# One product of 72 rows for forget sums and masks, and four gate tiles moved from the prompt to the decode

## The reference

```
u = RMSNorm(x);  z = u @ W_in          # q, k, v, forget gates, branch gates, merge gates mg
A (FoX, 8 heads):  s = q.k * scale + cum[query] - cum[key];  causal;  softmax;  @ v
B (NSA, 8 heads in 2 kv groups):  compressed + selected + window branches
   selected: importance per block of 64 keys (33 blocks), the 16 best are kept per token and group;
             a key of a block that is not kept gets -1e30 before the softmax
h = x + (sigmoid(g_A) * (A @ U_A) + sigmoid(g_B) * (B @ U_B)) @ W_out     # g_A, g_B from mg
y = h + HierMoE(RMSNorm(h))
```

## Time and profile before

| | |
|---|---|
| median of 3 runs | 2335.61 us (2333.5 to 2337.6) |
| the profiled execution, its own time | 2339.91 us |
| its span | 2337.8 us |
| TensorE (PE) busy | 2035.8 us, 87% |
| weight loads (PEld) | 1242.2 us, 53% |
| VectorE (DVE), ScalarE (ACT) busy | 532.0 and 235.9 us |
| moved by DMA | 614.98 MB, mean 263 GB/s |

### The profile page before, as it was taken

The page is one execution under the profiler, slowest core; times in us unless marked ns, Lnnn a source line. Parts: engine busy times, 40 slices in busy tenths (PEclk is TensorE's granted clock), DMA queues, the critical chain, the costliest instruction groups (busy, mean ns, idle before and its releaser), DMA issues. The chain is left out here.

```text
span 2337.8 us, 33992 instructions
## 1 busy us (share of the span) xinstructions
PE 2035.8 (87%) x13747; PEld 1242.2 (53%) x13747; DVE 532.0 (23%) x1099; ACT 235.9 (10%) x621; POOL 108.0 (5%) x124
## 2 busy tenths in 40 slices
PE   7999999999999999899999889999836786868773
PEld 7887677777767774454555556753322232323321
DVE  3545112223333441111111111100041111111112
ACT  0001111111102330000000011000000000000000
POOL 0000000000000000000000000000010211212111
PEclk9999999999999999999999999999967897888877
DMA  7664734332242229999999976323179999999998
GB/s 270 185 180 137 258 139 166 140 109 88 94 155 84 84 102 385 366 405 369 385 401 386 363 292 269 140 108 117 67 323 381 393 411 406 410 413 393 407 415 326
DMA packets 167986, 614.98 MB, mean 263 GB/s; under 512 B 31781, under 2 KB 89654, under 8 KB 132470
## 3 DMA queue, kind: packets, MB, share of 16 engines
q1 hardware_dynamic: 125742, 545.19, 60.1%
q0 software_dynamic: 22800, 45.07, 5.4%
q10 hardware_dynamic: 19288, 22.55, 3.0%
HBM read 702.95 MB, written 39.60 MB: 318 GB/s over the span
## 5 line engine op out<-in xcount | busy, mean ns | idle before, releaser
L511 PE MATMUL bank<-ut,wring 128*128 128x320 f32 x1408 | 385.6, 434 | 1.1 <-PEq L208 1.1
L511 PEld LDWEIGHTS bank<-ut,wring 128*128 128x128 f32 x1408 | 267.8, 191 | 112.0 <-issue 3.4
L1215 PE MATMUL bank<-ut,zt 128*128 128x320 f32 x576 | 180.2, 452 | 20.0 <-DMA zt<-in_w_gate 12.5
L2103 PE MATMUL bank<-wdn,par 128*32 128x512 f32 x512 | 88.7, 826 | 110.2 <-issue 108.8
L1215 PEld LDWEIGHTS bank<-ut,zt 128*128 128x128 f32 x576 | 103.1, 191 | 92.5 <-issue 46.4
L824 PE MATMUL bank<-ut,wring 128*128 128x320 f32 x448 | 144.4, 447 | 0.6 <-DVE ncum L1068 0.6
L2074 PE MATMUL bank<-wgu,arena 128*32 128x512 f32 x1024 | 119.9, 609 | 0.8 <-DVE arena L2154 0.8
L1542 PE MATMUL bank<-wring,arena 128*128 128x512 f32 x256 | 112.0, 595 | 3.1 <-DVE arena L1582 1.6
L674 DVE RECIPROCAL selmask<-selmask 128x320 f32<-128x320 f32 x30 | 64.5, 2149 | 201.3 <-ACT selmask L648 201.3
L824 PEld LDWEIGHTS bank<-ut,wring 128*128 128x128 f32 x448 | 80.8, 194 | 27.8 <-issue 7.9
L2103 PEld LDWEIGHTS bank<-wdn,par 128*32 128x32 f32 x512 | 18.2, 132 | 142.9 <-issue 141.1
(11 more groups left out here) (414 smaller groups left out, 2297.2 us busy)
## 6 DMA issues: line engine op xcount, KB each, us to landing
wgu<-in_w_gu SPq DMA_DIRECT2D x128, 1024.0 KB, 13.6
wdn<-in_w_dn SPq DMA_DIRECT2D x32, 2048.0 KB
arena<-in_kv_v SPq DMA_DIRECT2D x88, 640.0 KB, 8.6
arena<-in_kv_k SPq DMA_DIRECT2D x84, 640.0 KB, 9.1
wring<-in_w_proj SPq DMA_DIRECT2D x44, 1024.0 KB, 4.9
wring<-in_w_merge SPq DMA_DIRECT2D x32, 1024.0 KB, 4.9
wring<-in_kv_k SPq DMA_DIRECT2D x44, 640.0 KB, 9.3
wring<-in_kv_v SPq DMA_DIRECT2D x40, 640.0 KB, 9.4
```

The lines of the kernel that those rows point to most:

```text
L511: last = nc.tensor.matmul(m.bank[:, 2 + s % 2, 0:T], m.wring[:, s, k * P:(k + 1) * P], m.ut[:, k, :], start=(k == 0), stop=(k == KD - 1))
L1215: last = nc.tensor.matmul(m.bank[:, 7, 0:T], m.gw[n % 2][:, k // 2, k % 2 * P:(k % 2 + 1) * P], m.ut[:, k, :], start=(k == 0), stop=(k == ...
L2103: last = nc.tensor.matmul(m.bank[j * TW:(j + 1) * TW, 6 + i % 2, :], e.hid[:, i % 2, f * TW:(f + 1) * TW], w[:, f, cols:cols + 512], start ...
```

## The change

It does three things. (1) The score step has one product of 72 rows in place of the 16 products with `ncum` and the 4 with `maskq`: 64 rows are the turned sums (sequence, head) of a page's keys, and 8 rows tell a key's block within 512 keys. The stationary side, `extra`, is built on VectorE per sequence: ones for the sequence's own heads, and the masks of the step's 8 blocks. `ncum` is held as (page, b, head) and turned by 16 transposes and 4 copies, two on VectorE and two on ScalarE, into memory that the gate copies of the prompt used, so that both engines first wait for the stores of those. (2) The masks come out of 4 matmuls and one VectorE operation in `prompt_stage`. (3) NP is 10 in place of 14: 10 gate tiles in the prompt, 22 in the decode, and 5 matmuls of them after each step of scores and 4 after each of values.

```diff
-        self.blockof = self.selmask_all[0:NSB, :]
-        self.ncum = sb("ncum", P, NB, PAGES, FH)
+        self.cum_rows, self.block_rows = self.selmask_all[0:NB * FH, :], self.selmask_all[64:72, :]
+        self.ncum = sb("ncum", P, PAGES, NB, FH)
-        self.maskq = self.wflat[0:NSB, 7168:8192].rearrange("p (b j c) -> p b j c", b=NB, j=4)
+        self.masks = self.wflat[64:72, 7168:7168 + 4 * P]
+        self.spread = self.wflat[0:FH, 7680:7680 + FH * NT]
...
-NP = 14
+NP = 10
-SHARE = {"k": 4, "soft": 7, "v": 3}
+SHARE = {"k": 5, "soft": 7, "v": 4}
... prompt_stage, TensorE
-            done(nc.tensor.transpose(m.bank[0:NSB, 2, 0:P], rank, ident))
+            for q in range(4):
+                last = nc.tensor.matmul(m.bank[64:72, 2, q * P:(q + 1) * P], rank[:, 8 * q:8 * q + 8], ident,
+                                        start=True, stop=True)
+            done(last)
... prompt_stage, VectorE
-            nc.vector.memset(m.maskq, 0.0)
-            step(nc.vector.tensor_copy(selt[0:NSB, :], m.bank[0:NSB, 2, 0:P]))
-            for e in range(2):
-                for jj in range(2):
-                    last = nc.vector.tensor_scalar(
-                        m.maskq.rearrange("p b (g j) c -> p b g j c", g=G)[:, :, :, jj, 16 + 8 * e:24 + 8 * e],
-                        selt[0:NSB, :].rearrange("p (b g t) -> p b g t", b=NB, g=G), -NEG, NEG, ALU.mult, ALU.add)
-            step(last)
+            step(nc.vector.tensor_scalar(m.masks, m.bank[64:72, 2, :], -NEG, NEG, ALU.mult, ALU.add))
... decode_stage, SP
-            sp.dma_start(m.blockof, a["consts"][0:NSB, at:at + PAGES * P]).then_inc(m.rows_in, 16)
+            sp.dma_start(m.block_rows, a["consts"][64:72, at:at + PAGES * P]).then_inc(m.rows_in, 16)
... decode_stage, TensorE
-            for b in range(NB):
-                last = nc.tensor.transpose(m.bank[:, b // 4, (b % 4) * P:(b % 4 + 1) * P],
-                                           m.ncum[:, b, :, :].rearrange("p g h -> p (g h)"), ident)
+            for g in range(PAGES):
+                last = nc.tensor.transpose(m.bank[0:NB * FH, g // 4, (g % 4) * P:(g % 4 + 1) * P],
+                                           m.ncum[:, g, :, :].rearrange("p b h -> p (b h)"), ident)
... scores(b, q)
-                for i in range(4):
-                    for j in range(4):
-                        at = ((4 * q + i) * FH + 2 * j) * NT
-                        nc.tensor.matmul(m.bank[rows(j, 16), q, i * P:(i + 1) * P], spread[:, at:at + 16],
-                                         m.ncum[:, b, :, :].rearrange("p g h -> p (g h)"), start=False, stop=False)
                 for j in range(4):
-                    last = nc.tensor.matmul(m.bank[rows(j), q, :], m.maskq[:, b, j, :], m.blockof[:, q * 512:(q + 1) * 512],
-                                            start=False, stop=True)
+                    last = nc.tensor.matmul(m.bank[rows(j), q, :], extra[:, b % 2, q, j, :],
+                                            m.selmask_all[0:72, q * 512:(q + 1) * 512], start=False, stop=True)
...
-            pe.wait_ge(cum_ready, 3)
+            pe.wait_ge(cum_ready, 5)
... decode_stage, ScalarE
+            for s in range(2):
+                act.wait_ge(m.g_out[s], 16 * (NP // 2))
+            act.wait_ge(cum_turned, 1)
+            for x in range(2, 4):
+                nc.scalar.activation(m.cum_rows[:, x * 512:(x + 1) * 512], m.bank[0:NB * FH, x, :], ACT.Copy
+                                     ).then_inc(cum_ready, 1)
... decode_stage, VectorE, queries(b)
+                for e in range(2):
+                    nc.vector.tensor_copy(extra[0:NB * FH, b % 2, :, :, 8 * e:8 * e + 8],
+                                          bc(mine[:, :, e], NT).unsqueeze(1).broadcast_to([NB * FH, 4, 4, NT]))
+                    for jj in range(2):
+                        nc.vector.tensor_copy(extra[64:72, b % 2, :, :, 16 + 8 * e:24 + 8 * e].rearrange(
+                            "p q (g j) t -> p q g j t", g=G)[:, :, :, jj, :], masks[:, :, b, :, :])
... decode_stage, VectorE, its begin
             nc.vector.memset(qp, 0.0)
-            step(nc.vector.memset(pn, 0.0))
-            nc.vector.tensor_copy(spread.rearrange("p (n t) -> p n t", t=NT), bc(ident, NT)).then_inc(cum_ready, 1)
-            for b in range(2):
-                queries(b)
+            nc.vector.memset(pn, 0.0)
+            step(nc.vector.memset(m.snew_all[0:72, 512:1536], 0.0))
+            nc.vector.tensor_copy(m.spread.rearrange("p (n t) -> p n t", t=NT), bc(ident[0:FH, 0:FH], NT)).then_inc(cum_ready, 1)
+            queries(0)
+            for s in range(2):
+                dve.wait_ge(m.g_out[s], 16 * (NP // 2))
             dve.wait_ge(cum_turned, 1)
             for x in range(2):
-                nc.vector.tensor_copy(m.ncum[:, 4 * x:4 * x + 4, :, :].rearrange("p b g h -> p (b g h)"), m.bank[:, x, :]
-                                      ).then_inc(cum_ready, 1)
+                nc.vector.tensor_copy(m.cum_rows[:, x * 512:(x + 1) * 512], m.bank[0:NB * FH, x, :]).then_inc(cum_ready, 1)
+            queries(1)
```

More of the change, by code:

```diff
@@ L182, in __init__ @@
                          (self.onsa[:, :, :].rearrange("p h t -> p (h t)"), a[:, 12800:KVS * 1024]))
-        in_ncum = Pieces(self.ncum[:, :, :, :].rearrange("p b g h -> p (b g h)"))
+        in_ncum = Pieces(self.ncum[:, :, :, :].rearrange("p g b h -> p (g b h)"))
         self.ckt, self.part, self.hidp = in_ncum(P, G * TP), in_ncum(P, 256), in_ncum(P, 2, CW)
@@ L769, in prompt_stage @@
         (V_QSAMPLE, V_LFTOK, V_MAX, V_SHIFT, V_SUM, V_RECIP, V_PROBS, V_PCT, V_SCORE, V_FORCED,
-         V_CMP, V_TIES, V_ABOVE, V_RANK, V_SEL, V_SELT, V_MASK, V_CMPO, V_PAGESUM, V_NCN) = range(1, 21)
-        V_PAST = 21
+         V_CMP, V_TIES, V_ABOVE, V_RANK, V_SEL, V_SELT, V_CMPO, V_PAGESUM, V_NCN) = range(1, 20)
+        V_PAST = 20
         units = [(kind, h) for h in range(H) for kind in ("fox", "cmp", "slc", "win")]
@@ L1067, in _ @@
                 dve.wait_ge(pe_s, E_PAST + 2 * h + 1)
-                step(nc.vector.tensor_scalar(m.ncum[:, :, :, h], m.bank[:, (5, 1)[h % 2], 0:P].rearrange(
-                    "p (b g) -> p b g", b=NB), -1.0, None, ALU.mult))
+                step(nc.vector.tensor_scalar(m.ncum[:, :, :, h].rearrange("p g b -> p b g"), m.bank[
+                    :, (5, 1)[h % 2], 0:P].rearrange("p (b g) -> p b g", b=NB), -1.0, None, ALU.mult))
             chain = Chain(dve, back_step)
@@ L1128, in decode_stage @@
         in_vt = Pieces(m.vt[:, 0:2, :, :].rearrange("p a h d -> p (a h d)"))
-        spread = m.snew_all[:, 512:1536]
+        extra = m.snew_all[0:72, 512:1536].rearrange("p (s q j c) -> p s q j c", s=2, q=4, j=4)
         pt, ptw, ptn = in_arena(P, PAGES, P), in_arena(P, 4, P), in_arena(P, 2, P)
@@ L1256, in new_scores @@
                 for j in range(4):
-                    nc.tensor.matmul(m.bank[rows(j, 16), 4, 0:NT], spread[0:FH, 16 * j:16 * j + 16],
+                    nc.tensor.matmul(m.bank[rows(j, 16), 4, 0:NT], m.spread[:, 16 * j:16 * j + 16],
                                      m.ncn[:, b * NT:(b + 1) * NT], start=False, stop=False)
@@ L1390, in queries @@
                 q = qp[:, b % 2, :].rearrange("p (j c) -> p j c", j=4)
+                mine = ident[0:NB * FH, b * FH:(b + 1) * FH].rearrange("p (j e) -> p j e", e=2)
+                masks = m.masks.rearrange("p (q b g t) -> p q b g t", q=4, b=NB, g=G)
+                for e in range(2):
[4 more added lines that the diff above has]
+                            "p q (g j) t -> p q g j t", g=G)[:, :, :, jj, :], masks[:, :, b, :, :])
                 nc.vector.tensor_scalar(q[:, :, 0:80].rearrange("p j (e c) -> p j e c", e=2)[:, :, :, 0:NT],
@@ L2244, in shape_constants @@
     key = np.arange(PAGES * P)
-    c["blockof"] = np.pad((key[None, :] // SELB == j[:, None]).astype(float), ((0, P - NSB), (0, 0)))
+    c["blockof"] = np.pad((key[None, :] // SELB % 8 == np.arange(8)[:, None]).astype(float), ((64, P - 72), (0, 0)))
     return np.ascontiguousarray(np.concatenate([np.asarray(c[n]).reshape(P, w) for n, w in C_LAYOUT], axis=1),
```

1 line of the change is left out of this document (removed).

## The result

The changed kernel takes 2363.98 us (median of 4 runs, 2357.1 to 2367.82) against 2335.1 for runs of the kernel before taken beside it: a ratio of 1.0121 with a 95% interval of 1.0103 to 1.0139. It is 29 us slower. The forecast was 2317 and the range ended at 2331. The profiled execution took 2367.82 us with a span of 2366.0.

A forecast was written before the change was run, and what follows sets the result against it. TensorE was taken to bound the prompt's attention, the DMA engines the decode. Terms -34.4 + 1.5 + 0.8 + 11.7 + 1.0 + 0.5 = -18.9 us from 2335.6 gave 2316.7, say 2317; range 2305 to 2331.

The forecast's parts named there:

- The prompt, -32.1 us: Prompt stage: four tiles leave, -34.4 us; VectorE's chain comes late, +1.5; masks by four matmuls, +0.8.
- +1.5: Prompt's attention: time lost because VectorE's chain falls behind TensorE within a head, at most 5.4 us over eight heads.
- The score step, 6.36 to 6.48 us: Decode: TensorE's time per score step after the change, 0.45 to 0.57 us less than 6.93.
- the 0.12 us that the sum took off each step: Decode score step: the last 8 records take 0.87 us at the other records' rate, at worst the 0.99 of now.
- The begin, +1.0: Decode's begin: the first key set is freed about 1 us later while the queue is empty, +1.0 us.
- I take the DMA side: Decode: four more tiles, 4.85 MB at 415 GB/s, cost +11.7 us when no gap takes them up.
- 475 of 538 us: Decode: time the queue's 197.18 MB would take at 415 GB/s, out of the stretch from 866 to 1404.
- the 13.2 of decode, begin and end together: Decode's forecast growth: transfers +11.7 us, later begin +1.0, and the last step's further gate matmul at the end +0.5.
- B: Decode: gate weights come late more often, 5 further waits of 3.1 us, half hidden, +8: 2325 us; chance 0.14.
- D: Decode: late weights in "soft" stop ring and DMA engines, 4.3 us per wait; six further waits give 2343 us; chance 0.06.
- rival A: Decode: DMA dips take up the new transfers, growth is TensorE's 2.7 us plus 0.5 at the end: 2308 us; chance 0.20.

The follow-up runs named there:

- the right column of the table: Decode spans with SP handling done gate tiles ahead of key/value loads: kernel before 508.1 us, 72-row product alone 504.4, moved tiles alone 528.4, both 518.0.
- the left column: Decode spans with SP's order as it was: kernel before 531.7 us, 72-row product alone 519.9, moved tiles alone 578.4, both 587.6.

## Why the prediction was wrong, step by step

- *The prompt, -32.1 us.* Right: -32.4. VectorE's wait for TensorE fell from 40.8 us to 13.5, where under 10 was forecast; TensorE is busy 98% of the stretch, and it waits 1.8 us for VectorE's chain where +1.5 was forecast. Eight times 0.7 is 5.6 us, not the 5.4 of the prediction; nothing hangs on it.

```profile
L1076 DVE TENSOR_TENSOR arena<-bank,arena 128x384 f32<-128x384 f32 (+1 forms) x32 | 14.9, 464 | 13.5 <-PE bank L912 10.1 <-PE bank L909 3.5
```

- *The score step, 6.36 to 6.48 us.* Right, at the worse end: 6.46. The 8 records of 72 rows take 0.97, not 0.87, so of the 0.12 us that the sum took off each step only 0.02 came. The Trainium skill (TensorEngine Tiling (Array Packing), Key Properties) says that a change of the tiling mode drains TensorE; no run here shows a price of such a change over those 0.02 us a step. The rows answer to the earlier trace rows.

```profile
872.63 2.78 PE L1229 MATMUL bank<-arena,wring 128*32 128x512 f32 x24 [0.56 <-DMA arena<-in_kv_k]
875.23 1.04 PE L1234 MATMUL bank<-selmask,snew 72*32 72x512 f32 x8
876.20 2.96 PE L1211 MATMUL bank<-ut,zt 128*128 128x320 f32 x10
879.09 0.38 PE L1245 MATMUL bank<-zt,wring 128*32 128x8 f32 x24
```

- *The begin, +1.0.* Right: the scores begin 6.1 us behind the first transpose where it was 5.3, and no wait of TensorE for the new copies shows.
- *The decode, "I take the DMA side", +11.7.* This step failed. It took the DMA engines' share of 0.99 for a bound and read the waits for weights as its shadow. That share is of one window of 65 us; over the whole decode it was 0.96 at 370 GB/s, and the prediction's own 475 of 538 us left 63 us of gaps. The share was high, but the order in which SP issues set when a transfer could start, and with 22 tiles that order left the engines idle. It measured +55.9 us for the 13.2 of decode, begin and end together. For a kernel whose weights come in time the term was sized well: four more tiles cost 13.6 us behind the new product in the right column of the table, against 12.2 with the end. There the whole change makes the decode 9.9 us longer and the time 14.5 shorter by the medians (2315.24 to 2300.7), near the forecast's 18.9: what was missed is the order of issue.
- *Rivals B and D.* The mechanism was theirs, D's in full: weights late, the ring full, the engines stopped, the clock halved behind it. D had 0.06, and even D ended at 2343. Two of its numbers were too small. Its 5 to 6 further waits were 8. By the places of the tiles, all nine that the prediction counted did wait. The other three are two that end in the last score step, with the next but one in the second values, and one that ends in "soft", with the next but one in the third values; following the queue past `load_set` would have shown that the loads of the first two start only after the first values. The kernel before has one wait of this kind already, its longest, 3.90 us, ended at 1133.6 us: the tile ended in the last score step and the next but one began in the third values. Two more of its four stand in "soft" (ended at 982.3 and 1305.6), where by D's own words no set is free, so what was held against D was no argument. And each wait was priced at 3.1 us from the earlier trace rows, a mean for 16 matmuls out of 35, but measured 5.4; that with 16 out of 43 and a shorter step the load has less time fits this, and isn't tested alone. For the priced 1.2 us of lower clock per wait, 27.0/12 = 2.3 came.
- *"the gaps come at fixed places, where SP waits for a free set and can't reach the gate loads behind"* stood in the prediction against rival A. It was the right observation, and was used for the wrong rival.

Why the product makes the late tiles worse (+9.2 us in the left column, -10.4 in the right) was shown only in its size. That shorter steps turn into longer waits fits the sums (37.9 to 65.4 us of waits); no run changes the length of a step alone.

## What to carry to other kernels

A filler product has a deadline of its own: before more of it is put into a stage, write down for each tile which instruction issues its load, what that instruction stands behind in its queue, and how long its place lies free. A queue that waits for a ring's place must not hold loads for another buffer that is already free; issuing those first was worth 63 us here, twice the 31 us that moving the tiles took from the prompt. A DMA share near 1 doesn't prove that transfers set the stage: the decode before had 0.96, and the order of issue alone took 23.6 us from it.

## What the runs showed of the hardware

With weights in time one core's DMA engines moved 389 to 390 GB/s as a mean over a stage of 504 to 518 us, at a share of 1.00. The same 5057 TensorE records of the decode took 479.3 us at a mean granted clock of 0.99 and 506.3 at 0.91, where 12 stops of 2.6 to 8.5 us lay between them. Loads of 1 MB issued on a second queue landed in 20.1 us (median) beside 11.3 to 14.2 us loads of 640 KB on the first, where on one queue they took 14.6.
